# Scores of two attention mixers as three products of rounded parts

## The chip, the cores and the metric

One core of a Trainium2 chip runs the whole program. The metric is the device time in microseconds, the median of the runs. An engine's row names are PE for TensorE (PEld for its weight loads), DVE for VectorE, ACT for ScalarE, POOL for GpSimd and SP for SyncE.

## The reference

512 tokens of width 1024 go through two blocks of one kind and one of another. A block of the first kind is a gated feed-forward layer, four attention mixers of 256 features side by side, an output projection and a second feed-forward layer. The change lies in two of the mixers, in both layers.

```python
# latent mixer: 4 heads, 64 plain and 32 rotated features; queries and keys come up from low-rank latents
q, k = rms_norm(q, mla_q_norm), rms_norm(k, mla_k_norm)        # (512, 4, 96)
p = softmax(q @ k.T * 96 ** -0.5);  y = p @ v
# difference mixer: 4 heads of two maps each, 32 features per map
q, k = rms_norm(q, diff_q_norm), rms_norm(k, diff_k_norm)      # (512, 8, 32)
p = softmax(q @ k.T * 32 ** -0.5 + t5_bias)
y = (p[0] - lam * p[1]) @ v
```

The other two are a neighbourhood mixer (16 x 8 windows of a 64-wide grid, 64 features a head) and a grouped-query mixer (64 features a head). The second kind of block (`second_block`) is not touched.

## The kernel before, in words

Activations lie feature by feature (`xT`, `h_hi`, `h_lo`: 8 tiles of 128 features by 512 tokens). A large product is made of rounded parts: `w_hi`, `h_hi` are operands rounded to `fp32r`, `w_lo`, `h_lo` what the rounding left, and three products hi x hi, lo x hi, hi x lo are added in a PSUM bank (`product`, line 1122). The score products of attention are single products of plain f32 operands (line 1438), and each stands in the trace as two instructions.

`project` computes the inputs of all four mixers, token by token, in ten weight panels. Normed queries and keys are then transposed on TensorE (`turn`, line 1314), and ScalarE copies them, with the gain as scale, from one of two PSUM banks into `qk_T`, 22 tiles of 512 columns that share their room with the weight panels (`turn_copy`, line 2190). The four turns of the difference mixer come between the products of the last panel, and its copies (lines 2227, 2228) between ScalarE's copies of the projection (line 2141).

`attention` runs through 40 pairs of (mixer, tile of 128 queries, two heads) in the order of `attention_pairs`, as steps of a pipeline: eight pairs of the neighbourhood mixer (steps 0 to 7), then difference and grouped-query pairs in turn (8 to 23), then two difference pairs and, from step 26, latent and difference pairs (latent at 26, 28, 30, 32 and 36 to 39). In step s the engines do, each in its own order:

- TensorE: the score products of pair s (line 1438), the transposes of the probabilities of pair s - 2 (line 1096), the mix with the values of pair s - 3 (line 1390), then a turn if one is due (line 1348). The turns of steps 6 to 13 bring the latents up (lines 1358, 1360), those of steps 17 to 24 turn latent queries and keys, 8 in all.
- ScalarE: the copy of the turn of step s - 1 (line 2217 for the latent mixer), the copy of the turned probabilities of pair s - 2 (line 2248), the two exponentials of pair s (line 2256).
- VectorE: bias and maximum of pair s (lines 3108, 3102), the difference of the two maps of pair s - 1 (lines 3086 to 3093), the result of pair s - 3 (lines 3120, 3133), sums for the norms.
- GpSimd: mask and bias before the stage, then, once the norm of the latents is known (step 15), scaling and rotating of latent queries and keys, four tiles (lines 1043 to 1057).

The two heads of a difference pair lie in different groups of 32 rows of the array, those of a grouped-query or neighbourhood pair in different groups of 64; a latent head takes 96 rows from row 0.

## Time and profile before

| | |
|---|---|
| runs | 2335.25, 2335.29, 2344.34 us; median 2335.29 |
| profiled execution | 2345.89 us, span 2344.1 us |
| granted TensorE clock, mean of the span | 0.992 |
| busy: TensorE, VectorE, ScalarE, GpSimd | 98%, 69%, 49%, 2% |
| attention of layer 0 | about 474 to 594 us of the span |
| attention of layer 1 | about 1453 to 1573 us of the span |

Busy time is the share of the span in which an engine had an instruction under way; on TensorE the durations of pipelined instructions overlap, so the distance between two starts is the better measure. All later rows are of this execution.

### The profile page before, as it was taken

Reading aid. Unit: us, or ns where it says so; the run is one execution under the profiler, and the core shown is the slowest. Engines: PE = TensorE matmul, PEld = TensorE weight load, DVE = VectorE, ACT = ScalarE, POOL = GpSimd, SP = SyncE. Lnnn points to the kernel's source line nnn. Section 1 sums busy time; section 2 is a strip of 40 time slices with the busy share of each in tenths; the row PEclk is TensorE's granted clock in tenths of the full one; section 3 lists DMA queues with packets and bytes.
Section 4 is the critical chain, followed back from the end, with each engine's and each line's share of the span. In section 5 each row is a group of like instructions: output and inputs, shape, how many; then the busy total and the mean of one; then the engine's idle time right before and its main releaser. Section 6 shows DMA issues by size and latency. Waiting matters only on the chain.

```text
span 2344.1 us, 41631 instructions
## 1 busy us (share of the span) xinstructions
PE 2304.2 (98%) x17180; PEld 1983.2 (85%) x17180; DVE 1609.8 (69%) x2531; ACT 1140.3 (49%) x1949; POOL 49.7 (2%) x68
## 2 busy tenths in 40 slices
PE   8999999999999999999999999999999999999998
PEld 6999998865789999889999887558899998788687
DVE  7957664578678668688668654875877576773644
ACT  4535344487445344535344445864444354444523
POOL 0000001010000000000000010200000000000000
PEclk9999999999999999999999999999999999999979
DMA  5333443210333334333334432003334233321001
GB/s 160 105 90 99 117 149 101 84 37 2 91 90 99 99 97 115 96 90 104 99 100 112 153 98 70 20 20 90 90 95 122 90 100 124 99 74 54 2 21 54
DMA packets 276139, 205.93 MB, mean 88 GB/s; under 512 B 10160, under 2 KB 263056, under 8 KB 275440
## 3 DMA queue, kind: packets, MB, share of 16 engines
q1 hardware_dynamic: 275120, 195.96, 28.2%
q0 software_dynamic: 832, 7.33, 0.8%
q8 instruction: 136, 2.23, 0.4%
q14 instruction: 51, 0.42, 0.1%
HBM read 199.06 MB, written 2.10 MB: 86 GB/s over the span
## 4 chain that ended last, share of the span: by engine, by line
PE 88%; DVE 6%; ACT 2%; DVEq 2%; issue 1%; DMA 0%; SPq 0%; ACTq 0%
PE bank L1129 23%; PE bank L1221 10%; PE bank L1223 10%; PE bank L1222 10%; PE bank L1198 6%; PE bank L1199 6%; PE bank L1200 6%; PE bank L1407 4%; PE bank L1504 2%; PE bank L1438 2%; PE bank L1390 2%; PE bank L1747 1%; PE bank L1348 1%; PE bank L1096 1%; DVE top L3102 1%
## 5 line engine op out<-in xcount | busy, mean ns | idle before, releaser
L2581 DVE TENSOR_TENSOR w_lo<-raw,w_hi 128x2048 fp32r<-128x2048 f32 (+2 forms) x117 | 240.4, 2055 | 159.5 <-ACT w_hi L1934 159.3
L1934 ACT CAST w_hi<-raw 128x2048 fp32r<-128x2048 f32 (+2 forms) x118 | 202.0, 1712 | 182.0 <-PE bank L1200 90.3
L1198 PE MATMUL bank<-hid_hi,w_hi 128*128 128x512 f32 x704 | 274.7, 390 | 0.9 <-DVE xT L2822 0.9
L1199 PE MATMUL bank<-hid_lo,w_hi 128*128 128x512 f32 x704 | 274.3, 390 | 0.0
L1200 PE MATMUL bank<-hid_hi,w_lo 128*128 128x512 f32 x704 | 273.9, 389 | 0.0
L1221 PE MATMUL bank<-h_hi,w_hi 128*128 128x256 f32 x864 | 245.1, 284 | 2.0 <-DVE w_lo L2766 1.5
L1222 PE MATMUL bank<-h_lo,w_hi 128*128 128x256 f32 x864 | 244.5, 283 | 0.0
L1223 PE MATMUL bank<-h_hi,w_lo 128*128 128x256 f32 x864 | 244.5, 283 | 0.0
L2766 DVE TENSOR_TENSOR w_lo<-raw,w_hi 128x1024 fp32r<-128x1024 f32 x144 | 175.4, 1218 | 3.2 <-ACT w_hi L2006 3.2
L1221 PEld LDWEIGHTS bank<-h_hi,w_hi 128*128 128x128 f32 x864 | 165.7, 192 | 4.1 <-issue 1.7
L1222 PEld LDWEIGHTS bank<-h_lo,w_hi 128*128 128x128 f32 x864 | 165.7, 192 | 0.9
L1223 PEld LDWEIGHTS bank<-h_hi,w_lo 128*128 128x128 f32 x864 | 165.7, 192 | 0.0
L1129 PE MATMUL bank<-h_hi,w_hi 128*128 128x512 f32 x416 | 163.9, 394 | 0.2 <-DVE w_lo L3290 0.2
L1223 PE MATMUL bank<-ops_hi,more_lo 128*128 128x256 f32 x576 | 163.0, 283 | 0.0
L1221 PE MATMUL bank<-ops_hi,more_hi 128*128 128x256 f32 x576 | 162.9, 283 | 0.0
L1129 PE MATMUL bank<-h_hi,w_lo 128*128 128x512 f32 x416 | 162.0, 389 | 0.0
L1129 PE MATMUL bank<-h_lo,w_hi 128*128 128x512 f32 x416 | 161.9, 389 | 0.0
L1129 PE MATMUL bank<-w_hi,h_hi 128*128 128x512 f32 (+2 forms) x448 | 159.8, 357 | 0.0
L1129 PE MATMUL bank<-w_hi,h_lo 128*128 128x512 f32 (+2 forms) x448 | 158.3, 353 | 0.0
L1129 PE MATMUL bank<-w_lo,h_hi 128*128 128x512 f32 (+2 forms) x448 | 158.3, 353 | 0.0
L1198 PEld LDWEIGHTS bank<-hid_hi,w_hi 128*128 128x128 f32 x704 | 132.3, 188 | 28.8 <-issue 2.4
L1200 PEld LDWEIGHTS bank<-hid_hi,w_lo 128*128 128x128 f32 x704 | 132.2, 188 | 27.7
(495 smaller groups left out, 5454.5 us busy)
## 6 DMA issues: line engine op xcount, KB each, us to landing
raw<-in_ffn_w_up SPq DMA_DIRECT2D x88, 512.0 KB, 5.2
raw<-in_ffn_w_gate SPq DMA_DIRECT2D x87, 512.0 KB, 4.0
raw<-in_ffn_w_down SPq DMA_DIRECT2D x96, 384.0 KB, 3.7
raw<-in_w_in SPq DMA_DIRECT2D x60, 512.0 KB, 4.6
raw<-in_w_out SPq DMA_DIRECT2D x24, 512.0 KB, 4.4
raw<-in_ffn_w_down SPq DMA_DIRECT2D x16, 512.0 KB, 4.6
t_bias<-in_t_rel POOLq DMA_DIRECT2D x2, 1792.0 KB, 11.1
raw<-in_w_in SPq DMA_DIRECT2D x8, 416.0 KB, 3.7
```

Source lines behind the costliest of these rows:

```text
L1129: last = pe.matmul(to, left[a](k), right[b](k), start=(begin and k == 0 and a + b == 0), stop=(end and k == n - 1 and a == 1))
L1198: pe.matmul(to, hi(k), hid_hi[:, k, :], start=(k == 0), stop=False)
L1199: pe.matmul(to, hi(k), hid_lo[:, k, :], start=False, stop=False)
L1200: last = pe.matmul(to, lo(k), hid_hi[:, k, :], start=False, stop=(k == n - 1))
L1221: pe.matmul(columns_at(to), w_hi_[:, k, :], x_hi[:, k, :], start=(begin and k == 0), stop=False, skip_group_check=True)
L1222: pe.matmul(columns_at(to), w_hi_[:, k, :], x_lo[:, k, :], start=False, stop=False, skip_group_check=True)
L1223: last = pe.matmul(columns_at(to), w_lo_[:, k, :], x_hi[:, k, :], start=False, stop=(k == HALF_K - 1), skip_group_check=True)
L1390: last = pe.matmul(to[half * HD:(half + 1) * HD], share[:, half * HD:(half + 1) * HD], value, start=begin, stop=end)
L1407: last = pe.matmul(bank[d % 4], w[:, k, cut], h[:, k, :], start=(begin and k == ks[0] and w is hi and h is h_hi), stop=(end and k == ks[-1 ...
L1934: act.copy(w_hi[:, at, 0:n], raw[:, at, 0:n]).then_inc(hi_ready[at], 1)
L2581: dve.tensor_tensor(w_lo[:, at, 0:n], raw[:, at, 0:n], w_hi[:, at, 0:n].bitcast(F32), ALU.subtract)\
L2766: dve.tensor_tensor(w_lo[:, at, cut], raw[:, at, cut], w_hi[:, at, cut].bitcast(F32), ALU.subtract)\
```

## The change

The scores of the difference and latent mixers are computed as three products of rounded parts. For each turn ScalarE now writes the operand twice: the whole f32 value, and the value rounded to `fp32r`. GpSimd subtracts one from the other for the second part. Difference: four copies of 128x256 per turn instead of two, then four subtractions of 128x512 on GpSimd, ahead of its rotations. Latent: two copies of 96x256 for the whole values and one of 96x512 for the rounded ones, instead of one of 96x512, then two subtractions of 96x256 per turn, sixteen per layer, after the rotations. TensorE waits on `low_ready` before the first difference pairs of heads 0 and 4 (steps 8 and 24) and before the first latent pair (step 26), there for all subtractions. The products of a pair are issued term by term, the two heads in turn. The latent operands move into the room of the neighbourhood mixer's bias (`room_parts`), into tiles of `qk_T` and into `h_lo`; for that the first latent turn's copy waits on the maxima of step 8. Two semaphores of the latent norm are joined with those of the other norms.

```diff
@@ -446,9 +449,31 @@
         def gq_tile(l):
             return 4 - df_tile(l)
 
-        def mk_tile(l):
+        def diff_low(l):
 
             return 8 + 4 * (slot(l, PAN_OUT) == 0)
+
+        qk_parts = sb("qk_parts", [P, KF, S], F32R, work_at)
+        room_parts = sb("room_parts", [P, NA_ROOM // S, S], F32R, na_room_at)
+        room_rows = na_room[:, :].rearrange("p (h s) -> p h s", s=S)
+
+        def latent_high(side):
+
+            return room_parts[:, 0:HEADS] if side else qk_parts[:, MQ_T:MQ_T + HEADS]
+
+        def latent_whole(l, side, h):
+
+            if h < 2:
+                at = 8 + 4 * slot(l, PAN_OUT) + 2 * side
+                return qk_T[:, at:at + 2]
+            return spare[:, 0:2] if side else room_rows[:, HEADS:HEADS + 2]
+
+        def latent_low(l, side, h):
+
+            if h < 2:
+                at = 8 + 4 * slot(l, PAN_OUT) + 2 * side
+                return qk_parts[:, at:at + 2]
+            return h_lo[:, KD - 4:KD - 2] if side else room_parts[:, HEADS:HEADS + 2]
 
         lat_T = [qk_T[:, LAT_T, :], qk_T[:, LAT_T + 1, :], wide[:, T * IN_W:T * IN_W + S]]
         mix_rows = mixed[:, :, :, :].rearrange("p a t n -> p (a t n)").rearrange("p (j s) -> p j s", j=4)
...
@@ -1073,10 +1097,22 @@
                     last = pool.tensor_tensor(piece, piece, mask, ALU.add)
                 last.then_inc(bias_ready, 1)
                 pool.dma_start(first_gain[:, :], A["first_gain"][l + 1]).then_inc(layer_loaded, 16)
-                pool.wait_ge(lat_root, at_layer(l, 1, 1))
+                pool.wait_ge(turn_copied, at_layer(l, N_TP, turns_freed(turn_at("diff", T - 1))[1]))
+                for at in (0, 2, 1, 3):
+                    pool.tensor_tensor(qk_parts[:, diff_low(l) + at, :], qk_T[:, diff_low(l) + at, :],
+                                       qk_parts[:, df_tile(l) + at, :].bitcast(F32), ALU.subtract).then_inc(low_ready, 1)
+                pool.wait_ge(seg_root, at_layer(l, N_MEANS, N_MEANS))
                 for t in range(T):
                     latent_queries(l, t)
                     latent_keys(l, t)
+                for m in range(2 * T):
+                    t, side = divmod(m, 2)
+                    cut = slice(t * P, (t + 1) * P)
+                    pool.wait_ge(turn_copied, at_layer(l, N_TP, turns_freed(turn_at("mla", m))[1]))
+                    for h in range(0, HEADS, 2):
+                        last = pool.tensor_tensor(latent_low(l, side, h)[0:QKD, :, cut], latent_whole(l, side, h)[0:QKD, :, cut],
+                                                  latent_high(side)[0:QKD, h:h + 2, cut].bitcast(F32), ALU.subtract)
+                        last.then_inc(low_ready, 1)
 
 
         @block.tensor
...
@@ -1367,14 +1403,20 @@
                 if mixer == "na":
                     feat, keys = slice(h % 2 * HD, (h % 2 + 1) * HD), slice(NA_AT[i], NA_AT[i] + NA_W)
                     k = qk_T[feat, NA_T + 2 + h // 2, :].rearrange("f (r c) -> f r c", c=GRID_W)
-                    return qk_T[feat, NA_T + h // 2, cut], k[:, :, keys]
+                    return [(qk_T[feat, NA_T + h // 2, cut], k[:, :, keys])]
                 if mixer == "diff":
-                    q, k, b, n = df_tile(l) + h // 4, df_tile(l) + 2 + h // 4, h % 4 * DQK, DQK
-                elif mixer == "gqa":
-                    q, k, b, n = gq_tile(l) + h % 2, gq_tile(l) + 2, h // 2 * HD, HD
-                else:
-                    q, k, b, n = MQ_T + h, mk_tile(l) + h, 0, QKD
-                return qk_T[b:b + n, q, cut], qk_T[b:b + n, k, :]
+                    feat, q, k = slice(h % 4 * DQK, (h % 4 + 1) * DQK), h // 4, 2 + h // 4
+                    hi, lo = (qk_parts[feat, at:at + 4] for at in (df_tile(l), diff_low(l)))
+                    return rounded(hi[:, q, cut], lo[:, q, cut], hi[:, k], lo[:, k])
+                if mixer == "mla":
+                    hi = [latent_high(side)[0:QKD, h] for side in range(2)]
+                    lo = [latent_low(l, side, h)[0:QKD, h % 2] for side in range(2)]
+                    return rounded(hi[0][:, cut], lo[0][:, cut], hi[1], lo[1])
+                q, k, b, n = gq_tile(l) + h % 2, gq_tile(l) + 2, h // 2 * HD, HD
+                return [(qk_T[b:b + n, q, cut], qk_T[b:b + n, k, :])]
+
+            def rounded(q_hi, q_lo, k_hi, k_lo):
+                return [(q_hi, k_hi), (q_lo, k_hi), (q_hi, k_lo)]
 
             def values(mixer, h, t, i):
...
@@ -1433,9 +1475,16 @@
 
                             last = turn_at(mixer, 2 * T - 1 if mixer == "mla" else T - 1)
                             pe.wait_ge(turn_copied, at_layer(l, N_TP, turns_freed(last)[1]))
-                        for j, h in enumerate(heads):
-                            q, k = operands(l, mixer, h, i)
-                            pe.matmul(score_of(p, j), q, k, start=True, stop=True).then_inc(scores_done, 1)
+                        if mixer == "diff" and i == 0 and heads[0] % 4 == 0:
+                            pe.wait_ge(low_ready, at_layer(l, N_LOW, 2 * (heads[0] // 4 + 1)))
+                        if p == FIRST["mla"]:
+                            pe.wait_ge(low_ready, at_layer(l, N_LOW, N_LOW))
+                        terms = [operands(l, mixer, h, i) for h in heads]
+                        for n in range(len(terms[0])):
+                            for j in range(2):
+                                last = pe.matmul(score_of(p, j), *terms[j][n], start=(n == 0), stop=(n == len(terms[j]) - 1))
+                                if n == len(terms[j]) - 1:
+                                    last.then_inc(scores_done, 1)
                     p = step - TURN_LAG
                     if 0 <= p < N_P:
                         single = PAIRS[p][0] == "diff"
...
@@ -2213,9 +2262,12 @@
                 elif kind == "gqa":
                     last = act.copy(qk_T[:, gq_tile(l):gq_tile(l) + 3, cut], b[:, 0:3, :])
                 elif kind == "mla":
-                    o = mk_tile(l) if t % 2 else MQ_T
-                    last = act.activation(qk_T[0:QKD, o:o + HEADS, t // 2 * P:(t // 2 + 1) * P], b[0:QKD], ACT.Copy,
-                                          scale=col(("mla_q_col", "mla_k_col")[t % 2])[0:QKD])
+                    cut, gain = slice(t // 2 * P, (t // 2 + 1) * P), col(("mla_q_col", "mla_k_col")[t % 2])[0:QKD]
+                    if t == 0:
+                        act.wait_ge(max_ready, at_layer(l, 2 * N_P, 2 * (FIRST["diff"] + 1)))
+                    for h in (0, 2):
+                        act.activation(latent_whole(l, t % 2, h)[0:QKD, :, cut], b[0:QKD, h:h + 2], ACT.Copy, scale=gain)
+                    last = act.activation(latent_high(t % 2)[0:QKD, :, cut], b[0:QKD], ACT.Copy, scale=gain)
                 else:
                     o = NA_T if kind == "na" else df_tile(l)
                     q, to = b[:, 0:2, :], qk_T[:, o:o + 2, cut]
...
@@ -2224,8 +2276,14 @@
                         q = whole[:, 0:2 * P].rearrange("p (n w) -> p n w", w=w)
                         to = qk_T[:, o:o + 2, :].rearrange("p j (b n) -> p (j b) n", b=NA_B)[:, :, t * w:(t + 1) * w]
                         cut = slice(NA_TILE[t] * P, (NA_TILE[t] + 1) * P)
+                    if kind == "diff":
+                        for at in range(2):
+                            low = qk_T[:, diff_low(l) + 2 * at:diff_low(l) + 2 * at + 2, cut]
+                            act.activation(low, b[:, 2 * at:2 * at + 2, :], ACT.Copy, scale=col(kind + ("_q_norm", "_k_norm")[at]))
+                        to = qk_parts[:, o:o + 2, cut]
                     act.activation(to, q, ACT.Copy, scale=col(kind + "_q_norm"))
-                    last = act.activation(qk_T[:, o + 2:o + 4, cut], b[:, 2:4, :], ACT.Copy, scale=col(kind + "_k_norm"))
+                    to = (qk_parts if kind == "diff" else qk_T)[:, o + 2:o + 4, cut]
+                    last = act.activation(to, b[:, 2:4, :], ACT.Copy, scale=col(kind + "_k_norm"))
                 last.then_inc(turn_copied, 1)
 
             def attention(l):
...
@@ -2260,8 +2318,8 @@
 
                         act.nop().then_inc(hi_ready[slot(l, PAN_LAT)], 1)
                     if step == ML_ROOT:
-                        act.wait_ge(lat_mean, at_layer(l, 1, 1))
-                        inverse_root(lat_rs[:, :, :], lat_ms[:, :, :]).then_inc(lat_root, 1)
+                        act.wait_ge(seg_mean, at_layer(l, N_MEANS, N_MEANS))
+                        inverse_root(lat_rs[:, :, :], lat_ms[:, :, :]).then_inc(seg_root, 1)
                     for n, mixer in enumerate(MIXERS):
                         if step == TILE_END[mixer][-1] + GN_ROOT:
                             act.wait_ge(gn_mean, at_layer(l, len(MIXERS), n + 1))
```

## Rows read from the trace of the kernel before

**Rows 1.** The page: busy us, share and instructions of TensorE, and its clock in 40 slices.
```profile
PE 2304.2 (98%) x17180; PEld 1983.2 (85%) x17180; DVE 1609.8 (69%) x2531; ACT 1140.3 (49%) x1949; POOL 49.7 (2%) x68
...
PEclk9999999999999999999999999999999999999979
```

**Rows 2.** Windows: attention of both layers, steps 18 to 25, a late part.
```profile
core 0: us, PE busy (x) PEld busy (x) DVE busy (x) ACT busy (x) POOL busy (x), PEclk, DMA share, GB/s
461.00:514.00 53.00, 51.69 (x515) 34.03 (x515) 30.85 (x114) 42.02 (x119) 0.00 (x0) 1.00 0.08 21
514.00:592.00 78.00, 73.93 (x1023) 46.00 (x1020) 65.20 (x176) 60.98 (x137) 12.82 (x24) 1.00 0.05 16
1493.00:1571.00 78.00, 73.74 (x1014) 45.70 (x1010) 64.93 (x176) 61.11 (x138) 12.81 (x24) 1.00 0.05 16
523.60:547.98 24.38, 23.98 (x348) 15.68 (x346) 19.47 (x59) 21.40 (x50) 8.14 (x16) 1.00 0.01 2
2260.00:2290.00 30.00, 30.00 (x275) 21.60 (x276) 10.24 (x29) 8.94 (x55) 0.00 (x0) 0.50 0.11 36
```

**Rows 3.** Chain of waits, attention of layer 0: start us, us on the chain, what.
```profile
461.07 2.76 PE bank L1129 x12
...
489.38 1.06 PE bank L1438 x4
...
546.31 1.93 PE bank L1438 x4
...
558.32 1.91 PE bank L1438 x4
...
583.93 1.22 DVE top L3102
```

**Rows 4.** Groups of instructions by form, TensorE: the difference mixer's scores.
```profile
L1438 PE MATMUL bank<-work 32*128 32x512 f32 x128 | 36.1, 640 | 0.0
```

**Rows 5.** Timeline, ScalarE at the end of the projection: start us, us.
```profile
464.95 0.48 ACT L2228 ACTIVATE work<-bank,cols 128x256 f32<-128x256 f32 x1
465.31 0.49 ACT L2227 ACTIVATE work<-bank,cols 128x256 f32<-128x256 f32 x1
...
467.49 0.84 ACT L2141 ACTIVATE wide<-bank,rstd_tok 128x256 f32<-128x256 f32 x2 [1.32 <-PE bank L1129]
```

**Rows 6.** Timeline, ScalarE in steps 24 to 26.
```profile
541.96 0.68 ACT L2217 ACTIVATE work<-bank,cols 96x512 f32<-96x512 f32 x1
542.52 0.58 ACT L2248 COPY probsT<-bank 128x512 f32<-128x512 f32 x1
542.99 0.70 ACT L2256 ACTIVATE probs<-bank,top 128x512 f32<-128x512 f32 x1
...
544.33 0.70 ACT L2217 ACTIVATE work<-bank,cols 96x512 f32<-96x512 f32 x1
545.73 1.01 ACT L2248 COPY spare_lo<-bank 128x1024 f32<-128x1024 f32 x1 [0.71 <-PE bank L1096]
546.64 0.69 ACT L2256 ACTIVATE spare_hi<-bank,top 128x512 f32<-128x512 f32 x1
```

**Rows 7.** GpSimd: groups (busy us, mean ns, idle before), then the end of its timeline.
```profile
L1043 POOL TENSOR_TENSOR wide<-wide,lat_rs 128x384 f32<-128x384 f32 x8 | 7.0, 875 | 267.3 <-ACT lat_rs L1961 267.3
...
L1056 POOL TENSOR_TENSOR wide<-wide,lat_rs 128x256 f32<-128x256 f32 x8 | 4.9, 615 | 0.0
...
531.48 0.61 POOL L1056 TENSOR_TENSOR wide<-wide,lat_rs 128x256 f32<-128x256 f32 x1
```

**Rows 8.** Timeline, TensorE from the last latent turn to the first latent pair.
```profile
543.35 0.64 PE L1348 MATMUL bank<-ident,wide 128*96 128x128 f32 x4
...
546.24 1.98 PE L1438 MATMUL bank<-work 96*128 96x512 f32 x4
```

**Rows 9.** Line 3093 in 518 to 530 us, then 532 to 546: ns minimum/median/maximum.
```profile
L3093 DVE SCALAR_TENSOR_TENSOR probs<-probs,ratio x2: 485/767/1049, 528.7 to 529.1; 128x256 f32<-128x256 f32 x2
...
L3093 DVE SCALAR_TENSOR_TENSOR spare_hi<-spare_hi,ratio x2: 480/482/485, 541.0 to 541.4; 128x256 f32<-128x256 f32 x2
```

12 lines of the change are left out of this document (7 added, 5 removed).

## The prediction

> **What bounds the kernel now.** I read the page's shares first. TensorE is busy in nearly the whole span, at the full clock except near the end [rows 1]. The change touches only the attention stage of each of the two layers, so I went to the windows of that stage. The second layer repeats the first to 0.2 us in every column, so I work out one layer and double it. TensorE is busy for 51.7 of 53 us and then 73.9 of 78, and in the second stretch VectorE has 65.2 and ScalarE 61.0 of 78 [rows 2]. Four fifths busy leaves little cover, so the chain of waits has to say who ends what.
>
> The chain of waits has three stretches in a layer. From step 2 to step 15 it runs through TensorE alone, each score pair with its full length (step 8 stands in the rows). From step 18 to step 30 it is mostly TensorE (steps 26 and 30). From step 32 to the end it is VectorE's: its `top` reductions lead there while latent score pairs run beside them [rows 3]. What a score pair saves counts in the first two stretches and not in the third.
>
> **The score pairs.** A plain f32 product appears as two TensorE instructions (128 records for 64 difference products [rows 4]), so a pair of heads is four. A latent pair, 96 rows high, takes 1.93 us on the chain, a difference pair, whose heads lie in different groups of 32 rows, 1.06 [rows 3]. So two rounds run side by side cost 1.06 and four in a row 1.93: a round is (1.93 - 1.06) / 2 = 0.435, and 0.19 is fixed. A product of rounded operands takes 2.76 / 12 = 0.23 (the twelve before attention, [rows 3]). The changed latent pair is six rounds, 0.19 + 6 x 0.23 = 1.57, less by 0.36. The trace has no rounded product on fewer than 128 rows, so the difference pair is bounded: side by side 0.19 + 3 x 0.23 = 0.88 (less by 0.18), one after another 1.57 (more by 0.51). I take side by side, because the same groups of rows do it with f32 in the nearest row, and because the change issues the two heads in turn.
>
> **Gain in the first stretch.** Steps 8, 10, 12, 14 and 16 hold a difference pair each, four of them on TensorE's chain and the fifth at its end: 5 x 0.18 = 0.9 us.
>
> **ScalarE's whole values.** For the difference mixer eight activations of 128x256 are added, in two lots of four, behind the projection's copies. One costs 0.36 from start to start, a lot 1.4. Behind each lot ScalarE waits 1.32 us for TensorE [rows 5], so a lot is hidden but for 0.1. Without that wait both would cost 2.8. I take 0.1.
>
> For the latent mixer each of eight turn copies gets two activations of 96x256 before its one of 96x512. By the same 0.36 (the row has 128 partitions and the same columns) that is 0.71 per turn. They fall into steps 18 to 25, one in each. There ScalarE does, from start to start, the turn copy 0.56, the copy of turned probabilities 0.47 (difference) or 0.91 (the others), and the two exponentials 1.34 [rows 6]. Two steps are 2 x (0.56 + 1.34) + 0.47 + 0.91 = 5.18, and the eight steps 20.7 of a stretch of 24.38 (523.60 to 547.98, [rows 2]). ScalarE is idle for 3.7 us of it, always for TensorE's transposes. The change adds 8 x 0.71 = 5.7. Even if every idle moment is filled, the stretch takes 26.4: **ScalarE becomes the bound there, and the eight steps grow by 2.0 us**, while TensorE would have needed 0.7 less. The transposes can be on time: in two steps TensorE needs under 6.1 against ScalarE's 5.18 + 1.42 = 6.6.
>
> **GpSimd's second parts.** Before a latent score pair TensorE now waits for all sixteen subtractions. One is 96x256, and the nearest row, 128x256, takes 0.615 [rows 7]; bounds are that and the 0.875 of 384 columns. In the trace GpSimd ends its rotations at 532 us [rows 7], three turns after the first one was copied. It then needs 1.2 us per turn, while turns come one in 3 us (eight in the 24.38), so it has caught up well before the last. What counts is the last: its copies start at step 25. Up to there ScalarE has 7 x 1.90 + 4 x 0.47 + 3 x 0.91 = 17.9 of 20.73 us (523.60 to 544.33); with 7 x 0.71 it has 22.9, so the last copies start 2.2 later, at 546.5, and end at 547.8. Two subtractions and their waits end at 549.1. TensorE asked for that pair at 546.3 [rows 3, 8], so it starts 2.8 late, and being 0.36 shorter it ends 2.45 late. Behind the waiting pair stand the transposes of step 24, and behind them ScalarE's copy. With 0.875 for a subtraction it would be 3.0.
>
> The four subtractions of the difference mixer (128x512; from the columns of rows 7 about 1.1 us each, as 0.26 us per 128 columns are added) start at 474 and end before 480, and step 8 wants two of them at 489 [rows 3]. They are hidden by the neighbourhood steps. They do stand ahead of the rotations on GpSimd, but these wait for the latent norm of step 15 anyway (idle before them 267 us in two layers [rows 7]).
>
> GpSimd's work also meets VectorE's. Of VectorE's subtractions of the two maps, two took up to 1.05 us while GpSimd rotated, and 0.48 in quiet stretches [rows 9]. The new work lies where VectorE has some cover (19.5 of 24.4 busy [rows 2]). I take 0.3 us, with 0 and 4.5 as the ends. The Trainium skill (SBUF — State Buffer, "Who interferes with whom") has a rule that speaks against the change: a VectorE instruction with two SBUF inputs and a GpSimd instruction that reads SBUF shut each other out for a whole instruction. The trace agrees as far as 1.05 against 0.48 goes; were all sixteen new ones to hold VectorE for their whole length, it would be 16 x 0.615 = 9.8 us per layer.
>
> **Second and third stretch.** The latent pairs of steps 28 and 30 are on the chain: 2 x 0.36 = 0.7 saved. Behind them ScalarE and VectorE lead, and four latent pairs save nothing. ScalarE's new wait in the first latent turn asks for the score maxima of step 8, long past. The joined semaphores change no order.
>
> **Sum.** Per layer -0.9 + 0.1 + 2.45 + 0.3 - 0.7 = +1.2 us, two layers +2.4. The rows are from an execution of 2345.9 us (span 2344.1), which would become 2348.3. The median of the runs shown is 2335.3, so I predict **2337.7 us**. Why the two differ is in rows 2: from 2260 to 2290 the granted clock is 0.50 (1.2 GHz), after a part with many products of 64x64, and two of three timed runs were 9 us shorter. That part is untouched.
>
> **Rivals.**
> 1. *The extras find room.* If ScalarE's and GpSimd's work delayed nothing, only TensorE's gains would be left: on the chain 0.9 + 3 x 0.36 = 2.0 per layer, 2331.3; if everything saved counted (16 x 0.18 + 8 x 0.36 = 5.8 per layer), 2323.8. For it speaks that ScalarE is idle 3.7 us there; against it that 5.7 do not fit into 3.7. It decides if an activation of 96x256 costs below 0.23.
> 2. *Rounded products in two groups of rows run one after another.* Each difference pair then is 0.51 longer instead of 0.18 shorter. The first stretch loses 5 x 0.69 = 3.5, steps 18 to 25 nothing more (TensorE's two steps reach ScalarE's 6.6), later about two pairs on the chain 1.0: +5.7 per layer, 2346.7, and with all later ones on the chain 2350. That is the side of slower. For it: no row shows rounded products side by side. Against it: f32 ones are.
> 3. *GpSimd and VectorE hold each other up.* Eight meetings at 1.05 - 0.48 = 0.57 on the chain are 4.5 per layer, so 2337.7 + 8.4 = 2346. Against it: VectorE waits for TensorE's scores in these steps.
> 4. *The low clock near the end falls into the median run.* Then 2337.7 + 9 = 2347, and the change has no part in it.
>
> **How the numbers follow.** Forecast 0.50, the extras find room 0.17, and with all gains counted 0.04, one after another 0.10, GpSimd against VectorE 0.05, low clock 0.14. The low end of the range takes in most of the first rival, the high end the centres of the other three: **2330 to 2348**. What a measurement of this kernel can tell is about 0.5%, 11.7 us. Below 2323.6 lies only the full form of rival 1: 0.04. Above 2347 lie half of rivals 2, 3 and 4 and a rest of the forecast: 0.17. Between: 0.79.
>
> **What would show it.** Right: difference score pairs near 0.88 and latent pairs near 1.57 on the chain; ScalarE without idle time in steps 18 to 25 and that stretch 2 us longer; TensorE's wait before the first latent pair ended by GpSimd; no longer stretch at the end of the projection. Wrong: difference pairs of 1.5 us, VectorE's subtractions of 1 us in every step, or ScalarE with idle time left in steps 18 to 25. Most exposed is the count of what ScalarE can fill, since its idle time there depends on when TensorE's transposes come.

## The result: forecast and measurement

The changed kernel takes **2354.4 us** (median of 8 runs, 2352.07 to 2364.39), the kernel before beside it 2336.93 (8 runs). The ratio is 1.0067, 95% interval 1.0045 to 1.0090. Forecast were 2337.7 us, a range to 2348, and 0.17 for slower. The prediction was wrong: 17 us are lost where 2.4 were expected.

**The page after**, as [rows 1]. The shares hardly move, but the clock row has a dip in slices 10 and 27, which hold the attention of the two layers (59 us a slice), and none near the end.
```profile
PE 2301.5 (98%) x17276; PEld 1999.3 (85%) x17276; DVE 1616.7 (69%) x2531; ACT 1155.0 (49%) x1997; POOL 83.8 (4%) x108
...
PEclk9999999998999999999999999979999999999999
```

**Windows after**, as [rows 2]: before and in steps 18 to 25, from the first latent score pair on, the rest of attention, and the second layer from its first latent pair on.
```profile
core 0: us, PE busy (x) PEld busy (x) DVE busy (x) ACT busy (x) POOL busy (x), PEclk, DMA share, GB/s
...
525.50:551.70 26.20, 22.31 (x348) 15.85 (x348) 21.82 (x58) 26.20 (x65) 20.13 (x32) 0.99 0.01 3
551.70:567.50 15.80, 15.76 (x161) 11.76 (x161) 9.46 (x28) 7.69 (x21) 0.00 (x0) 0.58 0.00 1
567.50:601.70 34.20, 29.39 (x433) 21.97 (x431) 29.39 (x75) 25.16 (x54) 0.00 (x0) 1.00 0.02 5
...
1537.40:1558.00 20.60, 20.52 (x170) 15.01 (x170) 10.93 (x33) 9.08 (x24) 0.00 (x0) 0.51 0.00 1
```
ScalarE is busy for 26.20 of 26.20 us: it is the bound of steps 18 to 25, as forecast (26.4). Right behind, the granted clock is 0.58 of full speed over 15.8 us and, in the second layer, 0.51 over 20.6: mostly 1.2 GHz instead of 2.4. Below, such a stretch at 0.50 is called a fall of the clock. In windows of half a microsecond the first begins at 551.2 us and lasts 14 us, the second begins at 1537.7 and lasts 24. Before, it was 1.00 in all of attention [rows 2]. No term of the prediction has this.

**The chain of waits after**, as [rows 3].
```profile
491.58 0.89 PE bank L1485 x3
...
550.01 0.72 POOL qk_parts L1113
550.74 0.87 POOL h_lo L1113
551.75 2.90 PE bank L1485 x6
...
560.41 2.86 PE bank L1485 x6
...
567.56 1.59 PE bank L1485 x6
```
A difference pair takes 0.89 (forecast 0.88). A latent pair takes 1.59 at full clock (forecast 1.57) and 2.86 to 2.90 at the low one. GpSimd's last two subtractions end the wait before the first latent pair, as forecast.

**Timelines after**, as [rows 6 to 8]: GpSimd's difference subtractions, the VectorE operation beside them, ScalarE's last latent turn, and what TensorE waited for.
```profile
475.75 4.94 POOL L1102 TENSOR_TENSOR qk_parts<-work,qk_parts 128x512 fp32r<-128x512 f32 x4 [89.63 <-ACT qk_parts L2286]
...
478.33 1.16 DVE L3236 TENSOR_TENSOR lam<-lam,rows 128x1 f32<-128x1 f32 x1
...
548.33 0.68 ACT L2269 ACTIVATE work<-bank,cols 96x256 f32<-96x256 f32 x1
...
549.00 0.69 PE L1432 MATMUL bank<-wide,probsT 128*64 128x64 f32 x16
...
551.75 2.04 PE L1485 MATMUL bank<-room_parts,qk_parts 96*128 96x512 f32 x4 [2.06 <-POOL h_lo L1113]
...
579.24 0.73 PE L1132 MATMUL bank<-ident,spare_hi 64*128 64x64 f32 x8 [1.43 <-DVE spare_hi L3151]
```
The wait for GpSimd makes TensorE stand still for 2.06 us, in the midst of small transposes and mixes. Such an idle time of TensorE between two of its products is called a standstill below. Later, in step 33, it stands for 1.43 us until VectorE has the maps. In the kernel before that was 0.93, in both layers:
```profile
570.33 0.73 PE L1096 MATMUL bank<-ident,spare_hi 64*128 64x64 f32 x8 [0.93 <-DVE spare_hi L3093]
```

### The profile page after: what moved, and what is told of

Same layout as the page of the kernel before. It is cut to its first block, busy times and chain, and to the rows that moved or that the text cites. A ratio compares the mean times of both kernels' runs of the same rounds, so it can differ in the third digit from the quotient of the medians.

```text
span 2352.4 us, 41915 instructions
## 1 busy us (share of the span) xinstructions
PE 2301.5 (98%) x17276; PEld 1999.3 (85%) x17276; DVE 1616.7 (69%) x2531; ACT 1155.0 (49%) x1997; POOL 83.8 (4%) x108
## 4 chain that ended last, share of the span: by engine, by line
PE 86%; DVE 6%; ACT 5%; DVEq 2%; issue 1%; DMA 0%; POOL 0%; SPq 0%; POOLq 0%; ACTq 0%
PE bank L1165 23%; PE bank L1257 10%; PE bank L1259 10%; PE bank L1258 10%; PE bank L1234 6%; PE bank L1235 6%; PE bank L1236 6%; PE bank L1449 4%; PE bank L1485 2%; PE bank L1553 2%; PE bank L1432 2%; PE bank L1796 1%; PE bank L1132 1%; DVE w_lo L2639 1%; PE bank L1384 1%
```

## How the times are compared

The clock falls in some executions of one kernel and not in others, so medians jump between levels. In 146 executions of the kernel before, taken beside the experiments, 70 have a mean granted clock of 0.997 or more (median 2335.4 us), 69 have 0.991 to 0.993 (2347.6; in the profiled one this is a fall of 34 us near the end, part of which is in [rows 2]) and 7 have 0.985 or 0.986. None lies between these levels. For each kernel I therefore give the mean granted clock and the time reduced to clock 1.000: mean time less 1.64 us for each 0.001 of clock. The 1.64 is the slope within the kernels, fitted over all their runs. A reduced time is good to some 0.5 us, a mean clock of 10 to 12 executions to 0.001 (both from the scatter between executions).

A mean clock mixes falls in attention with the fall near the end, which comes or stays away by chance. The last column of the table is free of that: it counts the executions whose mean clock is one that none of the 146 has, 0.987 to 0.990, 0.994 to 0.996, or under 0.985. They have lost clock in a way that the kernel before does not. The count is a lower bound: the profiled execution of the changed kernel has both its falls in attention and none near the end, and its mean clock is 0.991.

| kernel | runs | median us | mean clock | reduced to 1.000 | runs at other levels |
|---|---|---|---|---|---|
| before | 146 | 2344.7 | 0.9949 | 2334.0 | 0 |
| after | 8 | 2354.4 | 0.9889 | 2337.6 | 3 |
| e1, third term waits | 10 | 2352.2 | 0.9899 | 2333.8 | 7 |
| e2, dummy products in the wait | 10 | 2355.2 | 0.9896 | 2337.9 | 5 |
| e3, before, wait of five | 10 | 2354.4 | 0.9901 | 2339.1 | 3 |
| e4, no whole values | 10 | 2353.9 | 0.9878 | 2331.9 | 5 |
| e5, difference only | 12 | 2340.7 | 0.9945 | 2333.1 | 9 |
| e6, latent only | 11 | 2359.6 | 0.9890 | 2339.3 | 4 |
| e7, third term, five dummies in step 33 | 12 | 2339.2 | 0.9962 | 2335.9 | 0 |
| e8, before, both maps awaited | 12 | 2342.5 | 0.9943 | 2333.9 | 4 |
| e9, third term, mix first | 12 | 2344.8 | 0.9918 | 2334.8 | 11 |
| e10, before, mix first | 12 | 2345.4 | 0.9942 | 2334.1 | 4 |
| e11, difference only, mix first | 12 | 2347.0 | 0.9923 | 2335.2 | 1 |
| e12, third term, fourth product | 12 | 2350.9 | 0.9940 | 2338.6 | 5 |
| e13, third term, three dummies | 12 | 2349.5 | 0.9937 | 2335.4 | 0 |
| e14, before, wait of four | 12 | 2353.5 | 0.9890 | 2336.9 | 7 |
| e15, before, dummies near the end | 12 | 2338.0 | 0.9978 | 2335.8 | 1 |
| e16, changed, all dummies | 12 | 2340.7 | 0.9987 | 2338.2 | 0 |

The change costs 3.6 us of work and waits, not far from the 2.4 forecast, and 0.006 of clock, about 10 us. (Of the eight executions beside it, only three, at 2344 us or more, had the time of one with the fall near the end, so their median is low and the difference of the medians larger.) What lets the clock fall is the question of the experiments. The theory: a standstill of TensorE among small products. The rival: the shortened pairs leave it too little work. Dummy products, below, are products of an identity matrix with itself whose results nobody uses.

## Experiments on the first standstill (step 26)

**e1, the third term waits.** The one wait for all second parts goes; the products that need them wait instead.
```diff
-                        if p == FIRST["mla"]:
-                            pe.wait_ge(low_ready, at_layer(l, N_LOW, N_LOW))
...
                         for n in range(len(terms[0])):
+                            if mixer == "mla" and i == 0 and n:
+                                pe.wait_ge(low_ready, at_layer(l, N_LOW, (T + 2 if n == 1 else N_LOW - 1) if heads[0] == 0 else N_LOW))
```


> The changed kernel with TensorE's wait for the last second parts moved from before the first latent pair to before its third term, which is the first to read them. Theory W (the 2.06 us for which TensorE stands still before that pair are followed by the granted clock of 0.50, and the clock costs more than the wait): TensorE stands still for under 0.5 us there, no stretch of clock 0.50 in either attention stage, each layer 2 us shorter by the wait and 3 to 6 us by the clock, 8 to 16 us less than the changed kernel's 2354, so 2338 to 2346. Rival S (the thinner work of steps 18 to 25, with ScalarE as the bound, or the rounded products on 32 and 96 rows lower the clock, whatever the wait): the low stretch stays, only 1 to 4 us less.

Ratio 1.0031 (1.0006 to 1.0056); the median of 2352.2 us is outside the 2338 to 2346 that the theory gave. Timeline of TensorE, then windows of the first layer before and in its fall, and of the fall in the second:
```profile
549.99 0.70 PE L1485 MATMUL bank<-room_parts,qk_parts 96*128 96x512 f32 x2 [0.40 <-ACT room_parts L2270]
...
573.25 0.73 PE L1132 MATMUL bank<-ident,spare_hi 64*128 64x64 f32 x8 [1.43 <-DVE spare_hi L3151]
```
```profile
550.00:574.50 24.50, 22.25 (x323) 16.45 (x325) 21.07 (x58) 19.09 (x45) 1.54 (x2) 1.00 0.01 2
574.50:584.70 10.20, 10.20 (x109) 7.83 (x105) 7.39 (x25) 5.75 (x15) 0.00 (x0) 0.51 0.01 2
1557.70:1578.10 20.40, 20.40 (x166) 14.86 (x166) 13.29 (x35) 10.96 (x25) 0.00 (x0) 0.50 0.00 1
```
The standstill is down to 0.40 us and the fall at step 26 is gone: the clock is 1.00 up to 574.5. All of the reduced time's loss is gone too (2333.8). But the clock now falls some 23 us later, one to two microseconds behind step 33's standstill of 1.43, in both layers, and the mean clock is hardly better than that of the changed kernel (0.9899 against 0.9889). So the fall at step 26 goes with the first standstill, and a second fall stands behind it.

**e2, dummy products in the wait.** The wait stays, with eight products ahead of it.
```diff
                         if p == FIRST["mla"]:
+                            for _ in range(8):
+                                pe.matmul(bank[MISC + 1][:, 0:P], ident[:, :], ident[:, :], start=True, stop=True)
                             pe.wait_ge(low_ready, at_layer(l, N_LOW, N_LOW))
```


> The changed kernel with eight products of the identity with itself, 128 columns, into a free bank, issued just before the wait for the second parts: the wait for GpSimd is as long as before, but TensorE works for about 1.7 of its 2.06 us. Theory W: the clock stays at 1.00, the first latent pair takes 1.6 instead of 2.86 us, 6 to 12 us less than 2354 although nothing comes earlier. Rival S: the clock falls all the same and the time stays at 2354.

Ratio 1.0055 (1.0033 to 1.0077). The median did not drop by the 6 to 12 us expected (2355.2). Timeline of TensorE, then windows: the first layer before and in its fall, the second layer.
```profile
550.15 2.02 PE L1482 MATMUL bank<-ident 128*128 128x128 f32 x16 [0.38 <-ACT room_parts L2272]
```
```profile
550.10:575.20 25.10, 22.86 (x316) 17.40 (x316) 20.16 (x54) 18.44 (x43) 1.57 (x2) 1.00 0.01 2
575.20:585.40 10.20, 10.20 (x124) 7.90 (x122) 7.48 (x26) 6.25 (x16) 0.00 (x0) 0.50 0.01 2
1536.00:1600.00 64.00, 58.71 (x773) 45.25 (x772) 48.48 (x128) 40.41 (x88) 0.00 (x0) 1.00 0.11 35
```
The eight dummy products stand as 16 instructions and leave 0.38 us of standstill ahead of them. As in e1, the fall at step 26 is gone in both layers, and the first layer has one of 10 us behind step 33. The second layer has none, though it stands still there for the same 1.43 us; so it shows the change's own work: from its first neighbourhood score to the start of its last mix 130.6 us (1459.47 to 1590.07), before 128.2 (1452.76 to 1580.98): +2.4 per layer, where +1.2 was forecast. (The reduced times give less, 3.6 us for both layers.)

**e3, the wait alone, in the kernel before.** Five subtractions of GpSimd's behind the last latent turn, and TensorE waits for them before the first latent pair.
```diff
+                pool.wait_ge(max_ready, at_layer(l, 2 * N_P, 2 * FIRST["diff"]))
+                pool.wait_ge(turn_copied, at_layer(l, N_TP, turns_freed(turn_at("mla", 2 * T - 1))[1]))
+                for n in range(WAITS):
+                    pool.tensor_tensor(na_room[:, n * S:n * S + PW], na_room[:, n * S + PW:(n + 1) * S],
+                                       na_room[:, n * S + PW:(n + 1) * S], ALU.subtract).then_inc(bias_ready, 1)
...
+                        if p == FIRST["mla"]:
+                            pe.wait_ge(bias_ready, at_layer(l, 1 + WAITS, 1 + WAITS))
```


> The kernel before with nothing of the change, but with five GpSimd subtractions of 128x256 after the last latent turn's copy (their results are not used), for which TensorE waits before the first latent pair: by the trace of before they end about 548.3, so TensorE stands still for about 2 us at step 26. Theory W: the clock falls to 0.50 for 10 to 25 us in both layers, and the kernel is 8 to 18 us slower than before. Rival S: no fall of the clock, at most the wait itself, 4 us slower than before.

Ratio 1.0049 (1.0018 to 1.0081), mean clock 0.9901 against 0.9949. Timeline of TensorE, then windows:
```profile
548.32 1.10 PE L1446 MATMUL bank<-work 96*128 96x512 f32 x2 [2.10 <-POOL na_bias L1084]
```
```profile
548.30:572.20 23.90, 23.88 (x184) 13.51 (x186) 12.33 (x36) 9.13 (x23) 0.00 (x0) 0.54 0.00 1
1538.30:1562.20 23.90, 23.90 (x184) 13.40 (x185) 12.23 (x36) 9.07 (x23) 0.00 (x0) 0.54 0.00 1
```
This is the decisive run for the first standstill: no product is changed, no pair is shorter, and 2.10 us of standstill bring the low clock of the changed kernel to about the same place in both layers. (Its falls begin 1.7 to 1.8 us behind the restart of TensorE and last 24 us.)

**e14, four instead of five.** `WAITS = 4`, nothing else.

> The kernel before with the added wait before the first latent pair, for four of GpSimd's subtractions instead of five: a standstill of about 1.5 us instead of 2.1. At equal clock +3 to +4 us (five: +5.1). Theory (the longer it stands, the more often the clock falls): mean granted clock 0.991 to 0.994, between that of the kernel before and 0.990 with five; median 2343 to 2352. Rival (any standstill over 1 us at this place does the same): mean 0.990 as with five.

Ratio 1.0044 (1.0017 to 1.0071), mean clock 0.9890: as low as with 2.10, so my graded theory fell. Timeline of TensorE in the second layer, then windows: the first layer from the first latent pair on, the second layer before and in its fall.
```profile
1528.22 1.95 PE L1446 MATMUL bank<-work 96*128 96x512 f32 x4 [1.35 <-POOL na_bias L1084]
...
1552.28 0.82 PE L1102 MATMUL bank<-ident,spare_hi 64*128 64x64 f32 x8 [0.94 <-DVE spare_hi L3101]
```
```profile
547.60:600.00 52.40, 49.19 (x652) 30.46 (x652) 40.91 (x111) 37.90 (x82) 0.00 (x0) 1.00 0.07 22
1528.20:1552.60 24.40, 23.05 (x284) 13.37 (x284) 19.04 (x54) 17.01 (x41) 0.00 (x0) 1.00 0.01 2
1552.60:1580.00 27.40, 27.34 (x210) 15.42 (x208) 15.48 (x42) 13.01 (x29) 0.00 (x0) 0.50 0.00 1
```
In this execution no fall comes right behind the 1.35 us, in either layer. The only one in attention begins 24 us later, behind step 33, whose standstill is the 0.94 us of the kernel before, and it lasts 27 us. So the added wait of 1.35 us costs as much clock as that of 2.10, but not at the same place: it can let the clock fall at a later standstill that the kernel before bears.

**e4, no whole values.** ScalarE's two additional copies per latent turn go, and GpSimd subtracts the rounded values from themselves: the latent second parts are zero, so two of three latent products add nothing to the scores.
```diff
-                    for h in (0, 2):
-                        act.activation(latent_whole(l, t % 2, h)[0:QKD, :, cut], b[0:QKD, h:h + 2], ACT.Copy, scale=gain)
```


> The changed kernel without ScalarE's whole values of the latent mixer: GpSimd subtracts the rounded value from itself, so that part of the computation is left out (the latent second parts are zero), while GpSimd's and TensorE's work stays. ScalarE is then no bound in steps 18 to 25. Theory W: TensorE reaches the first latent pair 3 to 4 us earlier in its layer; it still waits for the last two subtractions, about 1 us, and the clock stays up if that is short enough: 2332 to 2340. Rival S in its form that ScalarE's load lowers the clock: the same. In its form that rounded products lower the clock: the low stretch stays and the time is above 2345.

Ratio 1.0033 (1.0010 to 1.0057), reduced time 2331.9, which is 5.7 us under the changed kernel: 2.8 per layer are ScalarE's copies and the lateness behind them. TensorE's standstill before the first latent pair is 0.28 us. The clock still falls, in the profiled execution in the second layer behind step 33 (standstill 1.43), and the mean clock is the lowest of all (0.9878), so the median is far above the 2332 to 2340 expected.

**e5 and e6, one mixer each.** e5 has the changed difference scores with the latent part of the kernel before; e6 the reverse.
```diff
-N_LOW = T + 4 * T
+N_LOW = T          # e5;  4 * T in e6
...
```
The rest of the two edits puts the scores, copies and subtractions of the other mixer back as they were.


> Only the difference mixer's scores are three rounded products; the latent scores, their turn copies and GpSimd's work after the rotations are as in the kernel before. Of the steps of the prediction this keeps the gain of the first stretch (-0.9 us per layer), the 0.1 of the copies and the VectorE operation that GpSimd's subtractions held (+0.5), and takes away ScalarE's lateness and the standstill of TensorE before the first latent pair. Theory (single standstills of TensorE among sparse products let the granted clock fall): no fall at step 26; at step 33 TensorE stands 1.1 us instead of 0.93, since its score pair there is 0.17 shorter. At most one fall there; time at equal clock 0 to 1 us under the kernel before, median within 4 us of it. Rival (the clock falls because the shortened pairs leave TensorE with less work in all of this stretch): most of the shortened pairs are here (16 of 24), so the clock falls in attention as after the whole change, and the median is 6 us or more above the kernel before.

> Only the latent scores are three rounded products, with ScalarE's whole values and GpSimd's sixteen subtractions; the difference scores are as in the kernel before. ScalarE is full in steps 18 to 25 again. Theory (standstill): TensorE stands about 2 us before the first latent pair in both layers, the granted clock falls there for 14 to 24 us per layer; at equal clock +4 us against the kernel before (twice 2.45 and GpSimd's share, less 0.7 twice), median +7 to +12. Rival (it takes both mixers' shortened pairs): no fall at step 26 or later, median +2 to +4.

e5: ratio 0.9997 (0.9975 to 1.0018), reduced 2333.1. e6: 1.0062 (1.0036 to 1.0088), reduced 2339.3, TensorE standing 1.91 us before the first latent pair, with falls of 20 and 14 us there. The latent part alone costs as much work and clock as the whole change. But e5 is not free of falls in attention. Timeline of TensorE and window, second layer of e5:
```profile
1550.68 0.78 PE L1124 MATMUL bank<-ident,spare_hi 64*128 64x64 f32 x8 [1.10 <-DVE spare_hi L3138]
```
```profile
1551.20:1571.60 20.40, 20.40 (x176) 12.78 (x176) 12.82 (x37) 8.86 (x22) 0.00 (x0) 0.50 0.01 1
```
Nine of its twelve executions have a mean clock that the kernel before never has; seven of the nine, at 0.994 to 0.996, are too high to hold the fall near the end. Its mean over all (0.9945) is that of the kernel before only because at most three of the twelve met that fall, of the kernel before about half. Two thirds of the shortened pairs are in e5 and its standstill is only 1.10 us instead of 0.93, so the rival, less work of TensorE, is not out at step 33.

## Experiments on the second standstill (step 33)

**e7 and e13, dummy products there.** As e1, with five products (e7) or three (e13) before the wait for VectorE's maps.
```diff
+                        if step == FIRST["mla"] + 7:
+                            pe.wait_ge(probsT_ready, at_layer(l, N_P, p))
+                            for _ in range(5):
+                                pe.matmul(bank[PAIR_TURNED][:, 0:P], ident[:, :], ident[:, :], start=True, stop=True)
                         if single:
                             pe.wait_ge(pair_ready, at_layer(l, 2 * len(DIFF), 2 * DIFF.index(p) + 1))
```


> As the kernel in which the second and third products of the first latent pairs wait each for their own parts, and in addition, in step 33, five products of 128x128 with the identity before TensorE's transposes wait for VectorE's maps (they fill 1.26 of the 1.43 us for which TensorE stands there). Theory (standstill): no idle stretch of TensorE over 1.2 us is left between steps 8 and 36, the granted clock stays 1.00 there in both layers in most executions; median that of the kernel before within 3 us, mean granted clock that of the kernel before within 0.001. Rival (less work of TensorE in the whole stretch): the clock falls anyway near 575 or 585 us, the median stays 6 us above, as without the five products.

> As the kernel with five dummy products in step 33, but with three (0.8 us of the 1.43 are filled, 0.6 us of standstill are left). At equal clock 2334 to 2335, since five cost 2 us; no fall in attention, mean granted clock 0.995 or more, median 2335 to 2345, by whether the low clock near the end falls into it. Rival (all of the standstill must be filled): falls remain, mean 0.992 or less.

Ratios 1.0011 (0.9988 to 1.0033) and 1.0026 (1.0003 to 1.0049). Page, timeline of TensorE and windows (both layers from the first latent pair on) of e13:
```profile
PEclk9999999999999999999999999999999999999999
```
```profile
571.96 0.94 PE L1494 MATMUL bank<-ident 128*128 128x128 f32 x6
573.46 0.73 PE L1132 MATMUL bank<-ident,spare_hi 64*128 64x64 f32 x8 [0.57 <-DVE spare_hi L3155]
```
```profile
550.20:604.60 54.40, 49.87 (x698) 37.63 (x698) 44.70 (x118) 39.43 (x85) 1.53 (x2) 1.00 0.07 21
1530.10:1584.50 54.40, 49.93 (x698) 37.67 (x698) 44.76 (x118) 39.48 (x85) 1.57 (x2) 1.00 0.07 21
```
The mean clock of each of the 24 executions is either 0.998 to 1.000 or 0.991 to 0.992, the level of the one low stretch near the end. None has a level that needs a fall in attention, and the profiled executions of both kernels have none. (Of the twelve at 0.991 or 0.992 the mean alone can't tell one fall near the end from two in attention; it would be odd, though, if two came and never one.) Of e1's ten, eight lie between these levels or below them (0.985 to 0.990 and 0.995). e13's median is high, above the 2335 to 2345 expected, because eight of its twelve executions are at the lower level (e7: four). Three dummies cost 1.6 us of reduced time against e1, five 2.1. They fill the standstill and give TensorE work at once, so they don't tell the theory from the rival.

**e8 and e10, the standstill alone, in the kernel before.** In e8 the transposes of step 33 wait for both maps; in e10 the mix of that step is put ahead of the transposes.
```diff
-                            pe.wait_ge(pair_ready, at_layer(l, 2 * len(DIFF), 2 * DIFF.index(p) + 1))
+                            both = 1 if step == FIRST["mla"] + 7 else 0
+                            pe.wait_ge(pair_ready, at_layer(l, 2 * len(DIFF), 2 * DIFF.index(p) + 1 + both))
```
```diff
+                    for work in (mix_values, turn_probs) if step in (FIRST["mla"] + 7,) else (turn_probs, mix_values):
+                        work(step)
```


> The kernel before, with one wait changed: in step 33 TensorE's transposes wait for both of VectorE's maps instead of the first alone, so that TensorE stands about 1.4 us instead of 0.93. No score pair is shortened. By itself this delays the transposes by 0.45 us per layer, of which later work hides a part: 0.5 to 0.9 us in all. Theory (standstill): the granted clock falls behind it in about two of three layers, for 10 us or more each; mean granted clock 0.003 to 0.006 under the kernel before, median +5 to +9 us. Rival (less work of TensorE as such): the clock doesn't fall in attention; median within 1 us of the kernel before.

> The kernel before with the same swap in step 33: TensorE's 0.93 us of standstill are filled by the mix. The transposes start some 0.2 us later than now, the mix 1.6 us earlier. VectorE leads there, so at equal clock nothing to 0.5 us is gained per layer; the clock doesn't fall in attention before, so the median moves with the low clock near the end alone: within 3 us of the kernel before. Rival (later transposes delay the chain through ScalarE's copy): +0.5 to +1 us at equal clock.

Timelines of TensorE, e8 and then e10:
```profile
570.62 0.46 PE L1096 MATMUL bank<-ident,spare_hi 64*128 64x64 f32 x8 [1.32 <-DVE spare_hi L3094]
```
```profile
571.18 1.03 PE L1390 MATMUL bank<-wide,probsT 128*64 128x64 f32 x28 [1.61 <-DVE mixed L3126]
```
e8: ratio 1.0012 (0.9989 to 1.0036). e10: 1.0003 (0.9978 to 1.0027). e10 missed its purpose. I had counted on a mix that could start at once, but it waited for VectorE to take the mix before it, and the standstill grew to 1.61 us instead of vanishing. That makes it a second reading of the same question. The means, 0.9943 and 0.9942, are hardly under 0.9949, and both profiled executions have the clock at 1.00 in all of attention. But four of e8's twelve executions have the mean clock 0.989, and four of e10's 0.988, 0.990 and 0.994, levels that none of 146 executions of the kernel before shows. So in this place the kernel before bears 1.3 to 1.6 us of standstill mostly, but not always: a longer standstill alone does cost clock there in some executions. It does so less often than in e5 (four of twelve each against nine), where the standstill is shorter, 1.10 us, and the difference pairs are the shortened ones.

**e9 and e11, mix first in the changed kernels**: the same edit on e1 and on e5.

> The changed kernel with the waits of the first latent pairs put before the second and the third products, and in step 33 TensorE's mix with the values (step minus 3) ahead of its transposes (step minus 2): the mix, 1.44 us, is ready before and fills the 1.43 us of standstill with work that has to be done anyway. Theory (standstill): no idle stretch of TensorE over 1.2 us is left there, the granted clock stays 1.00 in attention in nearly all executions; the five dummy products' cost of 2 us (2335.9 against 2333.9 at equal clock) is gone, so at equal clock 2333 to 2334.5, and the median is within 3 us of the kernel before. Rival (it was the additional work of the dummy products that held the clock): the clock falls in attention in half of the executions or more, median 6 us or more above.

> The difference mixer alone in three rounded products, with the swap in step 33: the gain of the first stretch without the standstills. At equal clock 2332.5 to 2333.5 (0.5 to 1.5 us under the kernel before, as difference mixer alone has -0.8), the granted clock 1.00 in attention in nearly all executions, where without the swap two of three executions had lost 0.003 there; median 0 to 3 us under the kernel before. Rival: falls in attention remain, since the shortened pairs leave TensorE with less work; median 2 us or more above.

The standstill is 2.11 us in e9 and 1.78 in e11. Ratios 1.0018 (0.9992 to 1.0044) and 1.0022 (0.9995 to 1.0049), mean clocks 0.9918 and 0.9923. The mix waited for VectorE here too, so both missed their purpose and their forecasts (means of 1.00 in attention in nearly all executions). The profiled execution of e9 falls behind step 33 in both layers, for 10 us each, and that of e11 in the second, for 27 us. e11 against e5: with 1.78 us instead of 1.10 the mean clock is 0.9923 instead of 0.9945. e9 against e1: with 2.11 instead of 1.43 it is 0.9918 instead of 0.9899. Neither difference is clear of the scatter, and they point in opposite ways, so length alone doesn't order these kernels.

**e12, a fourth product.**
```diff
-                    return rounded(hi[0][:, cut], lo[0][:, cut], hi[1], lo[1])
+                    return rounded(hi[0][:, cut], lo[0][:, cut], hi[1], lo[1]) + [(lo[0][:, cut], lo[1])]
```


> As the kernel in which the second and third products of the first latent pairs wait each for their own parts, and every latent pair has a fourth product (second part times second part), so that it takes about 2.1 us instead of 1.57 (before: 1.93). TensorE has its work back in steps 26 to 39, without dummy products. Theory (amount of work around the standstill): falls in attention are rare, mean granted clock 0.994 to 0.996; at equal clock 2335 to 2336 (two latent pairs on the chain, 0.5 each, in both layers, above 2334.1); median 2338 to 2347. Rival (length of the standstill in step 33 alone): it stays at 1.2 to 1.4 us and the clock falls as often as with three products, mean 0.990, median 2352 to 2356.

Ratio 1.0027 (1.0003 to 1.0050), mean clock 0.9940 against e1's 0.9899. With the work back, the standstill of step 33 is 0.98 us and the clock is better, but the profiled execution still has a fall of 10 us, in the first layer behind these 0.98 us, and five of twelve executions have a mean clock that the kernel before never has, though its standstill is nearly the same (0.93). It costs 4.8 us of reduced time where I had expected 1 to 2; the cause was not looked for (more latent pairs on the way to the end than the two I counted per layer would do it). Since it changes length and work together, it shows only that the two together were part of what kept the clock.

## The fall near the end, and the change without the clock

**e15 and e16.** Two dummy products in each round of the recurrence near the end, in the kernel before (e15) and in e13 (e16).
```diff
+                        for _ in range(2):
+                            pe.matmul(bank[RW_SA][:, 0:P], ident[:, :], ident[:, :], start=True, stop=True)
                         pe.wait_ge(state_ready, g)
```


> The kernel before with two products of 128x128 by the identity in each round of the recurrence near the end, ahead of the wait for the state (0.58 us of standstill per round while 64x64 products run around it). Theory (standstills among sparse products let the clock fall): the fall of 34 us from 2258 us on is gone from nearly all executions, the mean granted clock is 0.998 or more, median 2334 to 2337, against 2338 to 2346. Rival (that fall has another cause): as frequent as before, median 2337 to 2347, or up to 4 us longer by the dummy products.

> The changed kernel with the first latent pairs' waits ahead of the second and third products, three dummy products in step 33, and the same two dummy products per round near the end. Theory: no fall anywhere in most executions; median 2335 to 2338, at most 2 us above the kernel before with the same dummy products: what the change is worth without the clock, 0 to +2 us. Rival for the change (its gains come out once nothing falls): 1 us or more under that kernel.

Windows of e15, the late part that was at 0.50 in [rows 2]:
```profile
2230.00:2290.00 60.00, 58.86 (x1316) 50.65 (x1313) 32.93 (x68) 21.04 (x72) 0.00 (x0) 1.00 0.07 22
```
e15: 2338.04 us, 2335.97 to 2348.44, with ten of twelve executions at 0.998 or more; ratio 0.9981 (0.9957 to 1.0005). e16: 2340.70, 2337.87 to 2342.32, and all twelve at 0.998 or more; ratio 0.9989 (0.9969 to 1.0010). The fall near the end is gone from nearly all executions, as the theory had it. Both medians are under that of the kernel before beside them, by 8 and 5 us (2345.96; 15 of its 23 executions have a mean clock of 0.993 or less). The intervals just take in 1, so neither is shown to be faster. In their comparison the clock is out of the way: e16 is 2.7 us the longer, the dummies of step 33 (1.6) included. So with the clock mended the change shows no gain; what is left above the dummies, 1.1 us, is hardly more than the scatter.

## Why the prediction was wrong

**What held.** The difference pair (0.88, measured 0.89), hence two groups of rows side by side and the second rival out. The latent pair (1.57, measured 1.59). ScalarE as the bound of steps 18 to 25 (26.4; measured 26.3, from the first whole value at 525.48 to the read-out of the last exponential at 551.74). GpSimd's subtractions as what TensorE waits for before the first latent pair. No loss at the end of the projection. Rival 1 is out, since a whole value of 96x256 takes 0.35 us from start to start (548.33 to 548.68), over its 0.23. Rival 4 is not it: the profiled execution after has no low stretch near the end, and takes 2354.2 us.

**Terms that were mis-sized.** From the first neighbourhood score to the first latent one it was 72.5 us before (473.73 to 546.24) and 76.3 after (475.43 to 551.75): +3.8 where the terms up to there gave some +2.3. Half a microsecond of it is gone by the first difference score (15.6 before, 16.1 after): GpSimd's subtractions of 1.23 us each, begun at 475.75, held VectorE's operation on `lam` for 1.16 us instead of 0.16. I had looked for such meetings at the rotations alone. The Trainium skill (SBUF — State Buffer, "Who interferes with whom") calls the pair of ports that these two engines share an exclusive lock; the trace agrees, a one-column operation waited for nearly a whole subtraction of 1.23 us. In e6, which has no difference subtractions, that stretch takes 15.6 us as before, and in e5, which has them, 16.1. The five shortened difference pairs bring 0.5 of the 0.9: from the first difference to the first latent score e5 takes 56.4 us, before 56.9. A subtraction of 96x256 takes 0.75 to 0.86 in the mean of its four groups, where I took 0.615. Of VectorE's maps (0.48 in quiet stretches; of the two in the first row of [rows 9] only one had 1.05), the six between 537 and 551 us, while these run, take 0.47 to 1.06 us, five of them 0.69 or more: that is rival 3, and the sign of it that I had named as wrong, in part. How much of it is on the chain no run separates. Together the change costs +2.4 us per layer (e2, second layer), not +1.2; the reduced times give +1.8. That alone would have given 2335.3 + 4.8 = 2340, inside the range.

**The step that failed** is the one after "so it starts 2.8 late, and being 0.36 shorter it ends 2.45 late". I priced the standstill at its own length. I had the clock in the sum for the part near the end, as a lottery with which "the change has no part in it", and looked at no other place where TensorE does small products between waits. The runs show in its place: the wait costs clock too. A standstill of 2.1 us before the first latent pair, put into the kernel before with nothing else changed, makes the granted clock fall behind it (e3), and the work that follows then runs for 14 to 24 us at 0.5; one of 1.35 us (e14) lowers the mean clock as much, with its fall behind step 33 in the execution that was profiled. Taking that standstill away (e1, e2) lets the fall come behind step 33, where the shortened pairs had lengthened the standstill from 0.93 to 1.43 and left TensorE less work around it. With dummy products there as well (e7, e13) no fall in attention is seen. In time this is some 10 us of clock in attention, a term that the sum had at nothing, beside 1.2 us of work and waits (3.6 against 2.4).

**What stays open.** Both the length of a standstill and the work around it count. Length alone, with the pairs of the kernel before, costs clock in e3, e14 and, in some executions, in e8 and e10. But at step 33 the shortened pairs matter as well. In the profiled executions of the kernels with shortened difference pairs and no fall at step 26 (e1, e2, e4, e5, e9, e11, e12) the clock falls behind step 33 in nine of fourteen layers, at standstills of 0.98 to 2.11 us. In those with the plain pairs (before, e8, e10, e15) it does in none of eight, at 0.93 to 1.61 us. What happened before counts too: e14 fell at 0.94 us, 24 us behind its added wait. And the same standstill lets the clock fall in one layer and not in the other (e2, e4, e5, e12). Nearest to shortened pairs at an unchanged standstill comes e12: its difference pairs are the shortened ones, its latent pairs slightly longer than in the kernel before, its standstill 0.98 us instead of 0.93, and it has falls that the kernel before never has. How much is due to length and how much to work isn't settled, and dummy products change both at once. The first 1.7 us of the profiled difference (first neighbourhood score at 473.73 before, 475.43 after) arise in the first 20 us. There the first products, up to 15 us, take 0.63 us each instead of 0.40, though the windows of the trace give a granted clock of 1.00 for both, so their reason stays open. It isn't the change: e15, whose products up to there are those of the kernel before, has them too and its first score at 475.23, and e6, with half of the change, has it at 473.72. One reading of the prediction was off, too, with nothing hanging on it: the two layers repeat each other to 0.3 us, not 0.2 [rows 2].

## What to carry to other kernels

A wait that makes TensorE stand still among small products can have two prices: its length, and a lower clock for what follows. Here the second was the larger, 7.9 us against 5.1 in e3 and 9.7 against 2.9 in e14. So look where the next standstill is before you shorten or remove one, and remember that faster products thin the work around it: in this kernel that seems to have cost clock too (e5). Spread a new wait over the products that need it instead of placing it ahead of all; where a standstill can't be avoided, a few dummy products in it may be cheaper than the clock. With a clock that falls in some executions only, compare mean clocks and times at one clock, or a median tells of the lottery; and look at the levels of the single executions, since a mean clock can hide a new fall behind an old one that happened to come less often (e5).

## What the hardware showed unexpectedly

- Standstills of 1.35 us (e14) and 2.10 us (e3) in each layer lower the mean clock alike, by 0.005 to 0.006. The Trainium skill (TensorE: Matmul & The Clock Gate, "A second HAM failure mode: psum-queue depth-cycling") tells of a kernel whose short idle moments between groups of products let the clock swing between its two levels, and that the loss is in the throughput. The traces agree in kind: the granted clock goes from 1.00 to 0.50 and back around standstills of one to two microseconds, with TensorE busy for 98% of the span, and some 10 us are lost to it.
- With the low clock, a latent pair of rounded products takes 2.90 us instead of 1.59.
- Six rounded products of 512 columns on 32 rows in two groups take 0.89 us, six on 96 rows 1.59.
- A VectorE operation of one column took 1.16 us beside a GpSimd subtraction of 1.23, and 0.16 without it.
- With two dummy products per round near the end two of 24 executions (e15, e16) have a mean clock under 0.998; of the kernel before more than half have (77 of 146).
- A fall can begin while TensorE still stands: in the first layer after the change at 551.2 us, 0.5 us before the restart. And it can come much later than the standstill that is new (e14, 24 us).
